# Query panels of the experts stage loaded as two transfers, of 120 and of 8 partitions

## What is computed

```python
def _peer(x, w_q, keys1, keys2, u, v):
    def one_chunk(xt):                                   # 128 tokens
        q = (xt @ w_q).reshape(BLOCK, PEER_HEADS, PEER_QDIM)       # 8 heads of 256
        s1 = jnp.einsum('chd,nd->chn', q[..., :half], keys1)       # 128 keys each
        s2 = jnp.einsum('chd,nd->chn', q[..., half:], keys2)
        ...
        ts, sel = lax.top_k(cand, PEER_TOPK)             # 16 of 256 pairs
        idx = jnp.take_along_axis(cidx, sel, axis=-1)    # 16 of 16384 experts
        g = jax.nn.softmax(ts, axis=-1)
        act = jax.nn.gelu(jnp.einsum('chkd,cd->chk', u[idx], xt))
        coef = g * act
        return jnp.einsum('chk,chkd->cd', coef, v[idx])
```

## Time and profile before

| | |
|---|---|
| median of 3 runs | 1484.42 us (1483.44 to 1485.96) |
| profiled execution | 1486.9 us, its span 1485.1 us |
| TensorE busy | 1330.0 us, 90% of the span |
| DVE busy | 826.3 us, 56% |
| ACT busy | 422.5 us, 28% |
| GpSimd busy | 292.9 us, 20% |
| gathers (queue 0) | 269.50 MB, 43.8% of 16 DMA engines' span |
| SyncE's transfers (queue 1) | 97.04 MB, 19.2% |
| mean granted clock of TensorE | 0.984 |

### The profile page before, as it was taken

The page is one execution under the profiler, slowest core; times in us unless marked ns, Lnnn a source line. Parts: engine busy times, 40 slices in busy tenths (PEclk is TensorE's granted clock), DMA queues, the critical chain, the costliest instruction groups (busy, mean ns, idle before and its releaser), DMA issues.

```text
span 1485.1 us, 19156 instructions
## 1 busy us (share of the span) xinstructions
PE 1330.0 (90%) x7308; PEld 879.7 (59%) x7308; DVE 826.3 (56%) x1996; ACT 422.5 (28%) x968; POOL 292.9 (20%) x269
## 2 busy tenths in 40 slices
PE   5999999999999999999999889999878787777777
PEld 2444799998578987888889654444323333332322
DVE  6406567445633344522214476777777777777654
ACT  1203321221153215455201234332322322222222
POOL 0000000000000010000000434545644344444430
PEclk9999999999999999999999999999999999999999
DMA  8343100054321523533245999999999999999995
GB/s 305 109 156 128 58 3 3 2 166 132 116 97 57 184 78 136 177 102 104 94 148 207 398 420 409 413 421 420 422 421 422 421 421 421 422 421 421 422 421 232
DMA packets 65111, 368.02 MB, mean 248 GB/s; under 512 B 7229, under 2 KB 8637, under 8 KB 31933
## 3 DMA queue, kind: packets, MB, share of 16 engines
q0 software_dynamic: 37152, 269.50, 43.8%
q1 hardware_dynamic: 27726, 97.04, 19.2%
q10 hardware_dynamic: 144, 0.26, 0.0%
HBM read 365.73 MB, written 1.05 MB: 247 GB/s over the span
## 4 chain that ended last, share of the span: by engine, by line
PE 63%; DMA 24%; DVE 9%; ACT 2%; issue 2%; another core or an unknown queue 0%; DVEq 0%; SPq 0%; ACTq 0%
PE bank L1605 15%; PE bank L2261 10%; DMA cst<-peer_in,arena 9%; PE bank L434 8%; DMA arena<-peer_in,arena 7%; DMA row<-peer_in,arena 5%; PE bank L2207 3%; PE bank L1150 3%; PE bank L536 3%; DMA ring<-peer_in,arena 2%; PE bank L1230 2%; PE bank L1207 2%; PE bank L1298 2%; PE bank L662 2%; DVE arena L2502 1%
## 5 line engine op out<-in xcount | busy, mean ns | idle before, releaser
L2261 PE MATMUL bank<-arena 128*128 128x512 f32 x584 | 272.5, 607 | 60.1 <-ACT arena L2365 57.3
L1605 PE MATMUL bank<-arena,ring 128*128 128x256 f32 (+2 forms) x1104 | 232.5, 371 | 5.5 <-DVE cst L2020 2.8
L2261 PEld LDWEIGHTS bank<-arena 128*128 128x128 f32 x584 | 109.0, 193 | 211.7 <-issue 211.3
L1605 PEld LDWEIGHTS bank<-arena,ring 128*128 128x128 f32 x1104 | 198.8, 190 | 34.5 <-DVE cst L2020 3.6
L2502 DVE CUSTOM_DVE_ANT_0 arena<-arena 128x1024 f32<-128x1024 f32 x146 | 177.0, 1223 | 52.9 <-DMA arena<-peer_in,arena 52.4
L2547 POOL DMA_INDIRECT arena<-peer_in,arena x146 | 164.1, 1124 | 179.3 <-PE bank L2261 153.9
L2365 ACT ACTIVATE arena<-cst,arena 128x128 f32<-128x128 f32 x256 | 88.9, 394 | 133.6 <-DVE arena L2451 132.0
L434 PE MATMUL bank<-ring,arena 128*128 128x512 f32 x256 | 114.7, 611 | 8.8 <-DVE arena L849 8.8
L2357 ACT ACTIVATE arena<-arena 128x2 f32<-128x2 f32 x129 | 38.0, 295 | 260.0 <-DVE arena L2502 259.9
L2261 PE MATMUL bank<-ring,arena 128*128 128x512 f32 x160 | 79.9, 645 | 21.4 <-ACT arena L2365 21.4
L434 PEld LDWEIGHTS bank<-ring,arena 128*128 128x128 f32 x256 | 50.0, 196 | 72.5 <-issue 72.5
(11 more groups left out here) (393 smaller groups left out, 1951.0 us busy)
## 6 DMA issues: line engine op xcount, KB each, us to landing
ring<-stream_in SPq DMA_DIRECT2D x155, 512.0 KB, 3.4
ring<-stream_in SPq DMA_DIRECT2D x8, 384.0 KB, 6.1
arena<-stream_in SPq DMA_DIRECT2D x6, 512.0 KB, 7.2
arena<-peer_in,arena POOLq DMA_INDIRECT x146, 32.2
row<-rows_in SPq DMA_DIRECT2D x4, 512.0 KB, 18.4
cst<-cst_in SPq DMA_DIRECT2D x1, 1933.0 KB, 17.5
res<-res_in SPq DMA_DIRECT2D x2, 544.0 KB, 4.1
row<-rows_in POOLq DMA_DIRECT2D x2, 512.0 KB, 6.5
```

What stands on the lines that cost most here:

```text
L1605: mm = nc.tensor.matmul(bank[:, first:first + width], slot[:, at + k * cols:at + (k + 1) * cols], src[:, k, :], start=k == 0, stop=k == kt ...
L2261: mm = nc.tensor.matmul(core.banks[2 * t + b][:, :], diag[i % ND], value_half(i, b), start=False, stop=last)
```

## The change

Each slot of the stream gets a list of partition ranges. It is the whole, 0 to 128, for all slots but the nine query panels; these have two ranges, 0 to 120 and 120 to 128. SyncE issues one transfer for each range, with the same semaphore, and TensorE's wait counts the transfers of this place so far.

```diff
@@ -259,6 +259,7 @@
         self.slot_freed = {}
         self.slots_issued = 0
+        self.loads = [[(0, P)] if key[0] != "wq" else [(0, P - 8), (P - 8, P)] for key, _ in self.slots]
@@ -305,7 +306,7 @@
         n = self.slot_no[key]
-        pe.wait_ge(self.slot_loaded[n % RING], 16 * (n // RING + 1))
+        pe.wait_ge(self.slot_loaded[n % RING], 16 * sum(len(self.loads[i]) for i in range(n % RING, n + 1, RING)))
         return self.ring[n % RING]
@@ -328,7 +329,8 @@
             src = stream[at:at + P * width].rearrange("(p w) -> p w", p=P)
-            sp.dma_start(self.ring[n % RING][:, 0:width], src).then_inc(self.slot_loaded[n % RING], 16)
+            for a, b in self.loads[n]:
+                sp.dma_start(self.ring[n % RING][a:b, 0:width], src[a:b, :]).then_inc(self.slot_loaded[n % RING], 16)
             self.slots_issued += 1
```

## The result

The changed kernel took 1494.84 us (median of 4 runs, 1493.21 to 1496.08) beside 1484.11 us (1483.44 to 1485.96) of the kernel before on the same chip. The ratio of the two is 1.0061, with a 95% interval of 1.0047 to 1.0074: **slower by 9.1 us, 7.0 to 11.0**. They are not quotients of the medians, so the two can differ by a microsecond or two; the medians here are 10.7 us apart.)

The account below looks back on a forecast made before the run. The gather stream was taken to bound the kernel, its last landing dated by one late DMA engine. 1484.4 us plus 0.8 us (5 panels x 0.156), or plus 0 if that engine stays, gave 1485.1 us, range 1478.3 to 1487.0.

Parts of the forecast that it names:

- What bounds the kernel: Experts stage: gathers saturate the DMA engines at about 421 GB/s; one engine working alone about 6 us dates the end.
- The prices: DMA engines: a row of 4,096 bytes takes 0.156 us of one engine, a panel of 128 rows 1.25 us.
- (a): Query panel loads: nine transfers of 128 partitions become nine of 120 and nine of 8; the bytes stay.
- (b): Deal over DMA engines: per panel one engine loses 1.25 us, eight gain 0.156 us, seven stay.
- (c): Query panels: the first four mostly pass before gathers queue up; 5 of nine count, bounds 4 and 9.
- (d): SyncE: 18 issues instead of 9, 0.33 us each, are hidden in its waits for TensorE.
- (e): TensorE: its panel wait asks for 32 instead of 16 in each slot; costs 0.
- (f): DMA engines: at most two more small completion packets per panel per engine; taken as 0, up to 0.1 us.
- The sum: Late engine at the stream's end: 5 panels x 0.156 = +0.8 us if it takes extra rows, 0 if it stays.
- the 6 to 7.5 that my forecast named as its sign: End of the stream: the lone engine still works 6 to 7.5 us after the rest, at 25 GB/s.
- The gain: Stream's end: the late engine is the one left out, so 1478.8 us (1478.4 to 1479.5); chance 0.30.
- The loss: DMA deal: 120 partitions go over eight engines, not fifteen; +6.2 us, 1490.6 us if the late one is among them; chance 0.07.

Follow-up runs that it names:

- e8: Kernel before plus 40 small transfers of 8 rows in the gather stream, into neighbouring partitions 0 to 7 of an unread tile; ratio 1.0140, +20.8 us.
- e7: Kernel before plus 40 small transfers of 8 rows in the gather stream, into partitions 0, 4, ... 28 of an unread tile; ratio 1.0033, +4.9 us.
- e6: Changed kernel with only the first four query panels split into 120 and 8 partitions, the rest whole; ratio 0.9990 to the kernel before, -1.5 us.
- e9: Changed kernel with only the last five query panels split into 120 and 8 partitions, the rest whole; ratio 1.0045 to the kernel before, +6.7 us.
- e5: Changed kernel with only the ninth query panel split into 120 and 8 partitions, the rest whole; ratio 1.0008 to the kernel before, +1.2 us.
- e2: Changed kernel with each query panel cut into two halves by columns, all 128 partitions each; ratio 0.9997 to the kernel before, -0.4 us.
- e10: Kernel before plus 40 small transfers of 7 rows in the gather stream, into partitions 0, 4, ... 24 of an unread tile; ratio 1.0032, +4.7 us.
- e1: Changed kernel with only the 120-partition transfers, the last 8 partitions of each query panel not loaded; ratio 1.0048 to the kernel before, +7.1 us.
- e3: Changed kernel with each query panel split into partitions 0 to 63 and 64 to 127; ratio 1.0049 to the kernel before, +7.3 us.

## Why the prediction was wrong

**What bounds the kernel** was right: the stream of gathers, ended by one late engine. (The prediction counts the slices from 0, its slice 22 is slice 23 above.) The forecast was no change to speak of, 1485.1; measured was a loss of 9.1 us.

**The prices** were the step that failed, in the words of the prediction "a row of 4,096 bytes takes 0.156 us of it and a panel of 128 rows, 8 rows an engine, 1.25 us". I took this price from transfers of 128 partitions and used it for transfers of 120 and of 8, as if a row cost the same wherever it goes. It takes 0.26 us after against 0.19 before over the first eight panels, and the gathers beside it are held up too: from 826 to 834 the whole stream moves 285 instead of 423 GB/s. In e8 against e7 nothing but the destination partitions differs, it is 16 us, and the gathers pay nearly all of it. I had written down that no row of before places such a transfer, but bounded only the number of rows on an engine, and put neither the time of a row nor what it does to the gathers beside it into the sum. Had a row of another shape been allowed twice its time, the bound would have been 5 x 1.25 = 6.2 us of every engine. What makes the rows of the nine panels slow is in part argued: that the written partitions alone can make a transfer dear is shown for 8 rows by e8, not for 120.

**(a), (b)** the deal was right: 15 + 8 engines, by the packets. **(c)** was right: the first four panels alone cost nothing (e6), the last five cost 6.7 us (e9). By the rates, in the 26 us from the first gather on, the engines move 386 GB/s before and 280 after (first row before, second after), 2.8 MB less or 6.5 us at 421 GB/s; the ninth panel's 2.0 us (profile of e5) make it 8.5.

```profile
816.55:842.55 26.00, 21.60 (x129) 18.96 (x128) 9.63 (x25) 7.68 (x17) 12.25 (x12) 0.93 0.99 386
```

```profile
814.16:840.16 26.00, 21.54 (x129) 18.89 (x128) 6.59 (x12) 6.86 (x14) 12.44 (x12) 0.93 1.03 280
```

**(d), (e), (f)**: nothing of them is seen. Two transfers a panel by columns cost -0.4 us (e2), and TensorE waits for no panel in the profile after: from 815 to 1485 us its waits name ACT (118.8 and 0.5 us), DVE (4.2) and issue (2.8).

**The sum** of +0.8 us for one row more a panel on the late engine fits what the end shows, 7 us alone instead of 6, and 8.5 + 0.8 = 9.3 us is near the measured 9.1. But the lone stretch is 6 to 7 us in e5 and e6 as well, and the interval of the loss is 4 us wide, so this term is not shown. The term left out is about ten times as large. The lone stretch of 7 us also lies inside the 6 to 7.5 that my forecast named as its sign: a true sign, which said nothing of the loss.

**The rivals.** *The gain* needed the late engine to be the one left out. It isn't: the lone stretch is still there in the profile after, and it is among those that carry a row in e7 and e10. So the gain was not to be had, whatever the rows cost. Fifteen of sixteen engines end within some 4 to 5 us of each other (1464 to 1469 us before), and one is late. That it sits at the end of the row of engines, for which I gave the gain more than the bare count, was my assumption: no run numbers the engines. Which of the seven it is, and whether the fetching of instructions makes it late, stays open: 18 packets of the instruction queue, 0.15 MB, run in the stretch after as before, but no run moved them. *The loss* got the sign and two thirds of the size, 6.2 us, for a cause that isn't there: the 120 partitions did go over fifteen engines. That was luck. Its place (the last five panels) was right, its mechanism was not, and 0.07 was too little for all the ways in which an unseen shape can be dear.

**What each piece costs.** The 120-partition transfers give 7.1 us (e1). The small ones are left with 1.9, which is inside the intervals. In e8 a transfer of 8 neighbouring partitions cost 20.8/40 = 0.5 us in all, 2.6 us for five, which agrees as far as the intervals go.

None of the kernels tried beats the kernel before.

## What to carry to other kernels

Beside a saturated stream, load a tile of 128 partitions with transfers of all 128 partitions, and if it must be cut, cut the columns: halves by columns were free here (rows of 2 KB; e2, -0.4 us), halves by partitions (e3, +7.3 us) cost as much as 120 + 8 (+9.1 us) within the noise. Read the DMA share and GB/s together: a share near 1 at half of the usual rate (0.99 at 227 GB/s, where the full stream has 421) was here the mark of the dear transfers, and the saturated stream beside such transfers paid too (285 GB/s where it was 423; in e8 79.91 MB of gathers where e7 has 85.78). Before you move bytes between DMA engines to relieve one that is late, find out with a few small extra transfers on a part of the engines whether it is among those that you relieve; and place what is slow where no one waits: the four panels ahead of the stream cost nothing that can be measured (e6, -1.5 us, -3.0 to 0.0).

## What the runs showed of the hardware

Forty transfers of 32 KB into partitions 0 to 7, in a saturated stream, cost 16 us more than the same bytes into partitions 0, 4, ... 28, or 0.4 us each (e8 against e7). From 814 to 818 us, with panels cut by partitions, the DMA engines moved 227 to 229 GB/s for 120 + 8, 221 to 223 for 120 alone, 227 to 236 for 64 + 64 and 225 to 250 for 112 + 16, at shares of 0.91 to 1.07; with the whole panels of the kernel before it was 272 to 276 at 0.84 to 0.94, and with panels cut by columns 273 to 286 at 0.82 to 0.89. What slows the rows that are cut by partitions, no run shows. A strided destination (every fourth partition) was no dearer than its rows: 40 x 0.156 = 6.2 us were expected for it, 4.9 (3.3 to 6.7) measured (e7). But SyncE took 0.62 us to issue one of these transfers, against 0.27 us for one into neighbouring partitions (first view e7, second e8; ns, min/median/max):

```profile
L2568 SPq DMA_DIRECT2D wide<-stream_in x40: 623/624/741, 879.8 to 1087.5; - x40
```

```profile
L2568 SPq DMA_DIRECT2D wide<-stream_in x40: 272/272/331, 880.1 to 1083.9; - x40
```

In this kernel one DMA engine worked on alone for some 5 to 8 us at the end of the stream, in every profile but that of e8, where it was 2 to 3 us.
